# Norm roots on four rows of 136 columns, spread by products into PSUM; earlier table loads; gated sample columns in PSUM

## What is computed

```python
def _rmsnorm(x, g):
    xf = x.astype(jnp.float32)
    y = xf * lax.rsqrt(jnp.mean(xf * xf, axis=-1, keepdims=True) + EPS)
    return (y * g.astype(jnp.float32)).astype(x.dtype)

for l in range(DEPTH):
    mod = (cs @ w_ada[l] + b_ada[l])[:, None, :]
    sh_m, sc_m, gt_m, sh_f, sc_f, gt_f = jnp.split(mod, 6, axis=-1)
    h = _rmsnorm(x, norm_mix[l]) * (1.0 + sc_m) + sh_m
    mix, (ng, nc, nr, nh) = _token_mixers(h, ...)
    x = x + gt_m * mix.astype(x.dtype)
    h = _rmsnorm(x, norm_ffn[l]) * (1.0 + sc_f) + sh_f
    x = x + gt_f * _swiglu(h, w_gate_up[l], w_down[l])
y = _rmsnorm(x, final_norm)
```

## Time and profile before

| | us |
|---|---|
| median of 3 runs | 2604.82 |
| lowest, highest | 2603.65, 2604.89 |
| the profiled execution | 2603.32 |
| its span, from the first to the last instruction | 2601.5 |

### The profile page before, as it was taken

One profiled execution on the slowest core, in us unless ns is written; L12 is line 12 of the kernel. 1 busy time (PEld: TensorE's weight loads), 2 busy tenths in 40 slices (PEclk: granted clock), 3 DMA queues, 4 the chain that ended last, 5 costly groups with the idle time before them and its releaser, 6 DMA issues. The chain is left out here.

```text
span 2601.5 us, 48595 instructions
## 1 busy us (share of the span) xinstructions
PE 2453.4 (94%) x19862; PEld 2343.9 (90%) x19862; DVE 1226.4 (47%) x1875; ACT 698.5 (27%) x1316; POOL 1412.9 (54%) x1140
## 2 busy tenths in 40 slices
PE   6989999989999999999979899999899998999997
PEld 4879898979998989999978799889899897999997
DVE  4654424241633566356356624241518435662653
ACT  3421223121012145145134222220210212550541
POOL 2553334557556835755855442446574576357565
PEclk8999999999999999999989899999999999999999
DMA  8730112312412723333365210142142242223322
GB/s 326 261 105 25 37 37 83 97 61 90 121 55 70 264 75 103 90 100 102 87 227 183 76 34 30 45 126 74 58 124 71 65 141 74 82 88 100 102 90 80
DMA packets 167053, 263.97 MB, mean 101 GB/s; under 512 B 14129, under 2 KB 83377, under 8 KB 165041
## 3 DMA queue, kind: packets, MB, share of 16 engines
q1 hardware_dynamic: 166832, 260.88, 31.2%
HBM read 239.65 MB, written 21.17 MB: 100 GB/s over the span
## 5 line engine op out<-in xcount | busy, mean ns | idle before, releaser
L956 PE MATMUL gemm_psum<-h_hi_lo,w_hi_lo 128*128 128x272 f32 x8352 | 1171.1, 298 | 40.6 <-DVE h_hi_lo L1547 32.3
L956 PEld LDWEIGHTS gemm_psum<-h_hi_lo,w_hi_lo 128*128 128x128 f32 x8352 | 1102.8, 195 | 85.9 <-issue 81.4
L634 POOL TENSOR_TENSOR w_hi_lo<-w_raw,consts 128x512 fp32r<-128x512 f32 (+1 forms) x476 | 519.2, 1091 | 841.1 <-PE gemm_psum L956 773.6
L625 POOL TENSOR_TENSOR w_hi_lo<-w_raw,w_hi_lo 128x512 fp32r<-128x512 f32 x546 | 735.6, 1347 | 198.7 <-ACT w_hi_lo L2337 161.4
L2337 ACT ACTIVATE tiles<-gemm_psum 128x544 f32<-128x544 f32 (+2 forms) x264 | 138.1, 526 | 685.8 <-PE gemm_psum L956 596.8
L956 PE MATMUL gemm_psum<-ffn_hi_lo,w_hi_lo 128*128 128x272 f32 x2112 | 265.2, 288 | 0.0
L956 PEld LDWEIGHTS gemm_psum<-ffn_hi_lo,w_hi_lo 128*128 128x128 f32 x2112 | 264.3, 188 | 0.8 <-POOL w_hi_lo L625 0.8
L986 PE MATMUL gemm_psum<-h_sums_hi_lo,w_hi_lo 128*128 128x272 f32 x1824 | 247.9, 288 | 0.0
L986 PEld LDWEIGHTS gemm_psum<-h_sums_hi_lo,w_hi_lo 128*128 128x128 f32 x1824 | 236.4, 188 | 0.0
L986 PE MATMUL gemm_psum<-h_hi_lo,w_hi_lo 128*128 128x272 f32 x1368 | 190.9, 289 | 0.0
L986 PEld LDWEIGHTS gemm_psum<-h_hi_lo,w_hi_lo 128*128 128x128 f32 x1368 | 179.2, 188 | 0.3
(11 more groups left out here) (267 smaller groups left out, 2627.0 us busy)
## 6 DMA issues: line engine op xcount, KB each, us to landing
tiles<-in_w_ada SPq DMA_DIRECT2D x64, 512.0 KB, 4.7
w_raw<-in_w_merge SPq DMA_DIRECT2D x96, 256.0 KB, 2.6
w_raw<-in_w_gu SPq DMA_DIRECT2D x96, 256.0 KB, 2.8
tiles<-in_w_gu SPq DMA_DIRECT2D x80, 256.0 KB, 3.0
w_raw<-in_w_first SPq DMA_DIRECT2D x68, 256.0 KB, 5.1
w_raw<-in_w_ret SPq DMA_DIRECT2D x64, 256.0 KB, 2.7
w_raw<-in_w_hg SPq DMA_DIRECT2D x64, 256.0 KB, 2.7
w_raw<-in_w_dn SPq DMA_DIRECT2D x64, 256.0 KB, 2.6
```

The source lines that it names most:

```text
L625: eng.tensor_tensor(lo_of(n), src, hi_of(n).bitcast(F32), ALU.subtract).then_inc(ready[n % SLOTS], 1)
L634: pool.tensor_tensor(hi_of(n), src, ones[:, 0:1].broadcast_to([P, words]), ALU.mult).then_inc(hi_done[n % SLOTS], 1)
L956: mm = pe.matmul(GP[:, 2 * SIDE[tile] + h, 0:HALF], whl[:, n % SLOTS, a, j * P:(j + 1) * P], rhs[:, b, step, h * HALF:(h + 1) * HALF], sta ...
```

## The change

The norm's sums go to four rows. `x_sums` multiplies with 32-column blocks of constants (`quarter_row`), each with ones in one column only, so that the sums of token columns 0 to 135 stand in row 0 of bank 0, those of 136 to 271 in row 1, and so on: 32x136, four products for the summed squares and four for the last square. The root and the reciprocal then run on 32x136 (`ROOT_ROWS`). A new step on TensorE, `root_spread`, multiplies the 32 rows with constants that select one row each (`sel`), four products of 136 columns, and so writes the reciprocal root to all 128 partitions in banks 0 and 1. VectorE waits for it, and the modulation and line 2861 read it there, in PSUM. Banks 0 and 1 are handed back after the modulation and no longer before it; the modulation ends with a wait for its own last product. The norm before layer 0 is kept, and its modulation reads SBUF.

In the layer-0 FFN norm the spread stands in TensorE's list between the conditioning's groups 2 and 3.

The Sqrt table is loaded ahead of the last square, before the wait for the last X tile. The Silu table of the FFN is loaded by an operation on one column ahead of the slabs `second`, and the last of these four slabs goes behind the first Silu.

`add_gated` writes the gated sample columns into unused columns of the tile's own `GP` bank instead of SBUF.

```diff
+    RSTD_PSUM = B[:, 0:2, 0:HALF]
+    QUARTER = T // 4
+    ROOT_ROWS = RWO[0:32, 0:QUARTER]
...
+                def quarter_row(i):
+
+                    o = C_HOT if i == 0 else C_HOT + 33 - i
+                    return C[:, o:o + 32]
+
                 def x_sums():
 
                     acquire(0)
                     acquire(1)
+                    out = B[0:32, 0, 0:QUARTER]
                     k.next(sig("x_summed"), KD - 2)
-                    for h in range(2):
-                        pe.matmul(B[:, h, 0:HALF], ones, sq_sum[:, h * HALF:(h + 1) * HALF], start=True, stop=False)
+                    for i in range(4):
+                        pe.matmul(out, quarter_row(i), sq_sum[:, i * QUARTER:(i + 1) * QUARTER], start=i == 0, stop=False)
                     k.next(sig("x_square"), KD)
-                    for h in range(2):
-                        mm = pe.matmul(B[:, h, 0:HALF], ones, sq_x[1][:, h * HALF:(h + 1) * HALF], start=False, stop=True)
+                    for i in range(4):
+                        mm = pe.matmul(out, quarter_row(i), sq_x[1][:, i * QUARTER:(i + 1) * QUARTER], start=False, stop=i == 3)
                     mm.then_inc(sig("x_sums"), 1)
+
+                def root_spread():
+
+                    k.next(sig("root_inverse"))
+                    for i in range(4):
+                        mm = pe.matmul(B[:, i // 2, i % 2 * QUARTER:(i % 2 + 1) * QUARTER], sel[0:32, i, :], ROOT_ROWS,
+                                       start=True, stop=True)
+                    mm.then_inc(sig("root_spread"), 1)
...
                 x_sums()
                 if ahead:
-                    for i in range(2, 4):
-                        ada_group_sum(i)
+                    ada_group_sum(2)
+                root_spread()
+                if ahead:
+                    ada_group_sum(3)
                     acquire(2)
...
                 drain(len(TILES), sig("act_ready"), KF)
                 x_sums()
+                root_spread()
...
                 def norm():
 
                     k.next(sig("root_ready"))
-                    release(0, 1)
-                    k.link(dve.reciprocal(RSTD, RSTD))
-                    k.settle()
+                    k.link(dve.reciprocal(ROOT_ROWS, ROOT_ROWS))
+                    say("root_inverse")
+                    k.next(sig("root_spread"))
...
-                def modulate(shift):
+                def modulate(shift, rstd):
...
                         dve.scalar_tensor_tensor(out=prompt(YP[i % 2]), in0=prompt(X[:, i, :]), scalar=SCG[:, i, 0:1],
-                                                 in1=prompt(RSTD), op0=ALU.mult, op1=ALU.mult).then_inc(sig("y_scaled"), 1)
+                                                 in1=rstd[:, :, 0:PH], op0=ALU.mult, op1=ALU.mult).then_inc(sig("y_scaled"), 1)
...
                     h_base[0] += KD
+                    dve.wait_ge(sig("h_ready"), h_base[0])
...
+                    gated = GP[:, 2 * SIDE[tile], HALF:HALF + SW]
-                    k.link(dve.tensor_tensor(SCT[:, :].rearrange("p (a b t) -> p a b t", a=2, b=4),
+                    k.link(dve.tensor_tensor(gated.rearrange("p (a b t) -> p a b t", a=2, b=4),
                                              by_seq(src[:, :, PH:HALF]), bc(g4.unsqueeze(3), [P, 2, 4, LS]), ALU.mult))
                     k.settle()
-                    k.link(dve.tensor_tensor(sample(xi), sample(xi), SCT[:, :].rearrange("p (a b) -> p a b", a=2), ALU.add))
+                    k.link(dve.tensor_tensor(sample(xi), sample(xi), gated.rearrange("p (a b) -> p a b", a=2), ALU.add))
...
-                modulate(0)
+                modulate(0, RSTD_PSUM if l else halves(RSTD))
+                for b in range(2):
+                    dve.nop().then_inc(free[b], 1)
...
                 norm()
-                modulate(3 * KD)
+                modulate(3 * KD, RSTD_PSUM)
+                release(0, 1)
...
+                def root_rows():
+                    k.next(sig("x_sums"))
+                    f(ROOT_ROWS, B[0:32, 0, 0:QUARTER], ACT.Sqrt, scale=1.0 / D, bias=epsc[0:32]).then_inc(sig("root_ready"), 1)
+
                 def x_squares():
 
                     for i in range(KD):
+                        if i == KD - 1:
+                            early_table()
                         k.next(sig("x_tile_ready"))
...
-                root(RSTD, 1.0 / D, "x_sums")
+                root_rows()
...
+                f(MISC[:, 6:7], epsc, ACT.Silu)
-                for n in second:
+                for n in second[0:3]:
                     high_slab(n)
                 plain_silu(0)
+                high_slab(second[3])
                 token_sums_hi(0)
...
-                dve.scalar_tensor_tensor(out=X[:, i, :], in0=X[:, i, :], scalar=FN[:, i:i + 1], in1=RSTD,
+                dve.scalar_tensor_tensor(out=halves(X[:, i, :]), in0=halves(X[:, i, :]), scalar=FN[:, i:i + 1], in1=RSTD_PSUM,
```

More of the change, by code:

```diff
@@ L758, in trunk @@
         "samples_ready", "stored_conv", "stored_prompt", "x_square", "x_summed", "x_sums", "x_tile_ready", "y_scaled", "h_full",
+        "root_inverse", "root_spread",
         "t_value", "t_hi", "t_ready", "sum_made", "s3_made", "p1_copied", "p5_copied", "u1_copied", "c11_done", "c12_done", "c21_done",
@@ L1533, in modulate @@
                     scaled(0)
-                    k.link(dve.tensor_tensor(split_samples(YS), columns(X), bc(sample(RSTD).unsqueeze(1), [P, KD, 2, SH]),
+                    k.link(dve.tensor_tensor(split_samples(YS), columns(X), bc(rstd[:, :, PH:HALF].unsqueeze(1), [P, KD, 2, SH]),
                                              ALU.mult))
@@ L1652, in drain @@
                     fill(10 ** 6, limit)
-                for b in range(4):
+                for b in range(2, 4):
                     dve.nop().then_inc(free[b], 1)
```

## The result

The change makes the kernel faster by 0.6%. Five runs of the changed kernel have a median of 2589.47 us (2588.97 to 2598.38) against 2604.82 before (now also five runs, 2603.65 to 2614.84); the ratio is 0.9938, with a 95% interval of 0.9918 to 0.9958, that is 11 to 21 us. The same kernel measured again beside the experiments gave 0.9941 (0.9927 to 0.9955). The forecast was 9.9 us, so 2594.9, with a range of 2589 to 2601. The median of the five runs lies just inside that range; by the ratio the change was about 16 us, so 2588.7, past the low end (which the forecast's working puts at 2588.6, 2589.8 less 1.2, and its text at 2589). Either way the gain was 5 to 6 us larger than forecast. The profiled execution took 2589.36 (span 2587.6) against 2603.32 (2601.5): 13.96 less. From here on the two profiled executions are compared.

The account below looks back on a forecast made before the run. TensorE is busy 94% of the span, so only its stops and lower clock leave something to gain. Terms +1.2-2.1-1.2-0.5-3.9-3.4 = -9.9 us, applied to 2604.82, give 2594.9; range 2589 to 2601.

Parts of the forecast that it names:

- The silu part: Behind each layer's first FFN pair: TensorE's stall falls from 2.75 to 0.78 (-3.9 in all), clock stays up (-3.4).
- The rival in which the clock falls all the same: Behind the shortened silu stalls TensorE's clock still drops, so the 3.4 is not gained: 2598.3 us; chance 0.22.
- Columns, Sqrt, root and reciprocal: At the norms: last sample add -0.64 (two norms), early Sqrt load -0.12, root -0.37, reciprocal -2.55, the last two by straight line.
- Square need a load of its own: Rival at three norms: Square undoes the early Sqrt load and Sqrt loads again, +4.2, 2599.1 us; chance 0.03.
- the spread's price at two norms: Spread with signals costs 1.6 at layer 0's end, 2.5 at layer-1 FFN and last norms, the last at half clock.
- The signals: Two signals between VectorE and TensorE around each spread, 0.40 us together, on top of its four products.
- 2.1 at the end of layer 0: Norm ending layer 0: savings on add, Sqrt load, root and reciprocal, less 1.6 for the spread, sum to -2.1.
- the layer-0 FFN norm, "+1.2": The spread pushes group 3, its copy and the joins in TensorE's queue, so the layer-0 FFN starts 1.2 later.
- the layer-0 FFN norm gains too: Rival: joins go through faster, so this norm gives -1.4 instead of +1.2, 2592.3 us; chance 0.08.
- VectorE's 1.4: At the layer-0 FFN norm the normed activations come 1.4 us earlier from VectorE.
- The spread one by one: Rival at all four norms: each spread record waits for the one ahead, 17.0 us more, 2611.9 us; chance 0.05.
- PSUM as a source: Scaling from PSUM costs the same as from SBUF; the skill's rule, 0.065 more a product, would give 2596.5 us.

Follow-up runs that it names:

- the part alone: Kernel before the change with only the early Silu table load and the fourth slab behind the first eviction: 2601.95 us against 2607.02, ratio 0.9972.
- the norm alone: Kernel before the change with only sums, root and reciprocal on four rows and the spread: 2604.64 us, ratio 0.9991.
- the control: The changed kernel unaltered, measured again beside the experiments: 2589.42 us against 2603.41 for the kernel before the change.
- the doubled spread: The changed kernel with the four products of each root_spread made twice into the same PSUM: 2597.28 us, one run, against 2601.99 before the change.

## Why the prediction was right or wrong

**The silu part was right, in mechanism and in size**: -7.3 forecast, -7.1 measured in the four silu stages of the changed kernel, and the same with the part alone. The stall fell to 0.58 where 0.78 was forecast, since the load was worth 1.42 and not 1.28, and the slab 0.74 and not half of 1.38. The clock gave 1.4 and 1.0 in the FFNs behind (1.5 each with the part alone), not twice 1.7. Another 0.6 in the layer-1 pair ahead of the stall belongs to the norm: the norm alone gave 0.9 there, the silu part alone nothing beyond the stall. That the two sums agree so closely is in part luck. The rival in which the clock falls all the same, held at 0.22, didn't happen.

**Columns, Sqrt, root and reciprocal were right**: 0.73 and 0.62 for 0.64; 0.09 to 0.13 for 0.12; 0.36 for 0.33; 0.99 for 1.00. The straight line through two rows far apart held. Nor did Square need a load of its own: in the changed kernel the Sqrt table is loaded at 915.15, the square at 920.48 runs behind it with no load in front. So that rival was wrong.

```profile
915.15 1.28 ACT L2363 ACT_TABLE_LOAD   x1
916.45 0.20 ACT L2363 ACTIVATE misc<-misc 128x1 f32<-128x1 f32 x1
920.48 0.66 ACT L2363 ACTIVATE tiles<-x 128x544 f32<-128x544 f32 x1 [3.83 <-DVEq L1600]
```

**The step that failed is the spread's price at two norms**, "1.6, 2.5, 2.5". The bounds (0.74 to 4.3) and 1.2 at full clock were right; measured 1.19. The signals were taken at 0.40 and cost 0.15 (1.34 from inverse to scaling). The error was to take the place of the clock's fall from one execution and to lay the new spread against it: at layer 1 the fall came 4.0 behind the last X tile in the kernel before (2195.57 to 2199.6), at about 7.0 in the changed kernel (2190.08 to 2197.1) and at about 3.9 in the control (2190.87 to 2194.8). The spread stands between, 4.7 behind the tile, so it is a matter of the execution: 1.34 or 2.33. Over the twelve kernels the fall came 3.9 to 4.3 behind that tile in seven and 6.8 to 7.1 in five, with and without the spread. (The control's place is from a granted clock of 0.70 from 2194 to 2196.) At the last norm the spread's records took 1.19 to 1.43 in all kernels but one. That is 1.2 of the error at each of the two: the last norm gave 2.1 where 0.5 was forecast, the layer-1 FFN norm 2.6 where 1.2 was. The rest, and the 3.0 for 2.1 at the end of layer 0, are small pieces on the chain: the gap between root and reciprocal shrank by 0.1 to 0.2 (0.26 to 0.03 at the end of layer 0), the sums by 0.1, and the signals.

Two things on that fall. At the last norm it may be more than the execution: the fall came 3.8 to 5.5 behind the last X tile in the four kernels without the spread and 5.4 to 6.7 in seven of the eight with it, where the spread starts 4.6 behind; whether the change moves it, and why, is open. And the forecast read the earlier trace rows as falls at 1315.2 and 2199.8; granted clocks of 0.77 and 0.80 over a us, between levels of 1 and 0.5, put them at 1315.5 and 2199.6, which leaves both spreads on the same side of them.

**The second step that failed is the layer-0 FFN norm, "+1.2"**. That the spread pushes group 3 and the joins through TensorE's queue is shown (the doubled spread costs 0.98 there). What the working left at its old value was the time of the joins, 5.54, of which it didn't ask at which clock they ran; the earlier trace rows had no row for that stretch. From 929.8 they ran at half clock (the fall there ended at 936.7), and with the spread between the groups they don't. From group 0 to the joins it is now 10.97 for 10.05, the spread's push; from the joins to the FFN 3.56 for 5.40; in all -0.9. The rival "the layer-0 FFN norm gains too" named that way, and got 0.08, since the joins running right up to the FFN was read as a reason against it; it says only that they are last, not that their length is fixed. It was the case that came, at -0.9 for its -1.4, with the other norms' error on top. But its size did not come from VectorE's 1.4: VectorE's first `h_hi_lo` tile was done at 932.0 and the FFN started at 933.56, right behind the joins, so TensorE's queue still ended last.

**The spread one by one** (2611.9) was wrong: the doubled spread adds 0.93 for eight more records, 0.12 each, where that rival needed 0.54.

**PSUM as a source.** The scaling takes 0.75 from PSUM (line 1546 above) as it did from SBUF. By the Trainium skill's rule ("VectorE: DVE Perf Modes", the TRN2 errata) it would, as an estimate, take 0.065 more; the trace doesn't show that, and the forecast was right not to add it.

What stays open: the edited stages gave 15.8 and the span 13.9, because the other two were 1.9 longer in this execution. The control shows 920.26 and 870.03 for the same two, so they move by over a us from execution to execution of one kernel. The first of them took 918.2 to 918.5 in the three kernels that have neither the columns nor the new norm, and 918.3 to 920.6 in the nine that have one, over 918.9 in all but one; the second 869.8 to 870.0 in the three and 866.4 to 872.9 in the nine. So a part of the 1.9 may belong to the change; these traces can't tell.

## What to carry to other kernels

A reciprocal over replicated rows is paid by its columns: moving it to a quarter of them and spreading the result with four small products took 2.56 off the reciprocal, 0.34 off the root, and put 1.34 on. Before a wait is costed at the head of a queue, look up the granted clock of every item in that queue, short matmuls too: an item at half clock has up to half its time to give back, and reordering alone can give it. And where a fall of the clock is to decide a price, look where it lies in more than one execution, and keep both prices.

## What the runs showed of the hardware

The order of work ahead of 32 short joins decided their clock: 3.7 us with the spread between the two groups of conditioning products, 5.3 to 5.6 without, in all of twelve profiled kernels. A longer idle of TensorE drew a fall behind it more often (2.75: seven of eight, 2.00: one of two, 1.32: none of two), but none did so always.

A VectorE product of the unedited convolution stage took 0.72 in the kernel before and 1.84 in the changed one, for 0.1 us in the order of two engines. Timeline of both engines, before:

```profile
209.32 0.72 DVE L1607 TENSOR_TENSOR tiles<-tiles 128x544 f32<-128x544 f32 x1 [0.22 <-DVE tiles L1598]
...
209.35 1.89 POOL L924 TENSOR_TENSOR tiles<-tiles,consts 128x544 f32<-128x544 f32 x1
```

and after:

```profile
209.83 1.35 POOL L928 TENSOR_TENSOR tiles<-tiles,consts 128x544 f32<-128x544 f32 x1
...
209.92 1.84 DVE L1630 TENSOR_TENSOR tiles<-tiles 128x544 f32<-128x544 f32 x1 [0.22 <-DVE tiles L1621]
```

Whichever began first ran at its own length and the other took longer by 0.5 to 1.1; TensorE's next wait grew with it from 1.43 to 2.35. It went either way in kernels that don't differ there: 1.8 to 1.9 in nine of the twelve, which all have a fall of the clock beginning at 182.5 to 184.7, and 0.72 or 0.73 in the three that don't have that fall. So both may be part of what moves the unedited stages; no run here separates them. The Trainium skill ("SBUF — State Buffer", Who interferes with whom) says of these two engines that a VectorE instruction with two SBUF inputs contends with a GpSimd instruction that reads SBUF, and that the order of issue decides which one blocks; the trace agrees (1.84 for 0.72, 1.89 for 1.35). The gated columns in PSUM took the same contention away: in the kernel before, the 7 sample adds without a GpSimd operation beside them took 0.19 and the 41 with one 0.57 to 1.0, a mean of 755 ns over all 48; it is 187 ns now, at most 191.
